# The first merge of DeltaNet's block inverse, done in 32x32 pieces on four row and column groups

## The chip, the cores and the metric

The kernel runs on one core of a Trainium2 chip. The metric is the device time of one launch in microseconds (us). Five engines of the core matter here: TensorE (PE for the matmul, PEld for loading its weights), VectorE (DVE), ScalarE (ACT), GpSimd (POOL) and SyncE (SP), which issues DMAs. Each works through its own list of instructions in order; semaphores tie them together. The time before the change is 1111.03 us, the median of 3 runs (1110.56 to 1111.17).

## The reference, cut to what matters

The program is a two-layer decoder trunk over 272 tokens (16 learned ones, 256 of the input) of width 1024: six sub-layers, four of them SwiGLU, one mixer of retention and gated DeltaNet heads, one of windowed and stick-breaking attention. The change is in the DeltaNet part of the first mixer. There the chunks of 64 tokens need the solution of a unit lower triangular system for each of four heads:

```python
a_mat = jnp.where(strict, jnp.einsum('bnhid,bnhjd->bnhij', k_beta, k) * decay, 0.0)
system = a_mat + jnp.eye(C, dtype=a_mat.dtype)
rhs = jnp.concatenate([v * beta[..., None], k_beta * jnp.exp(g_cum)[..., None]], axis=-1)
sol = lax.linalg.triangular_solve(system, rhs, left_side=True, lower=True, unit_diagonal=True)
```

and a scan over chunks that uses `sol`.

## The kernel before, in words

The kernel processes the DeltaNet tokens in chunks of 128 instead of 64, and inverts the triangular matrices instead of solving. Two chunks times four heads give eight matrices of 128x128 (index `q` from 0 to 7; a ninth holds the 16 last tokens of all heads). The 16x16 blocks on the diagonal are inverted on DVE (`block_inverses`). Then three merges double the block: 16 to 32 (`m == 0`), 32 to 64 (`m == 1`), 64 to 128 (`m == 2`). With X the inverse so far and E the part of the matrix that lies between two neighbouring blocks, a merge forms E·X (`merge_first`, PE), copies it from PSUM to the SBUF tile `w1` (`merge_copy`, ACT; `w1` is the buffer `dN`), forms X·(E·X) (`merge_second`, PE), and brings that into X (for `m == 0` an addition on DVE in `first_merged`, for the others a copy on ACT). The tile `XX` holds X in `XX[:, 0]` and its transpose in `XX[:, 1]`; DVE's 32x32 block transposes (`transposed`) make the second from the first.

In the first merge each of the eight matrices takes one matmul of 128x128 by 128x128 per product. `off_diag` is the matrix with a mask that leaves the 16x16 blocks E, so that all of the other entries multiplied are zeros. The results fill two PSUM banks for each product (4 and 5, then 6 and 7), four matrices in each. The second merge is already done in pieces of 32x32 (two for each matrix), whose results lie side by side in one bank (`merge_ps(1, bank)` is [128, 8, 32]; `merge_w1(1)` the same shape in `w1`).

The order of the work is written out by hand, one list for each engine. PE's list alternates projections (`proj(n, m)`: half a chunk of the mixer's input projection, 24 matmuls of 128x128 by 128x272, lines 1772 to 1774) and small DeltaNet matmuls (helper `mm`, line 1877), so that the second wait on other engines behind the first:

```python
proj(11, 0); merge_first(0); proj(11, 1); merge_second(0)
proj(12, 0); merge_first(1); proj(12, 1); merge_second(1)
proj(13, 0); merge_first(2); proj(13, 1)
```

A projection's weights are f32 and split in two parts: ACT makes the high part (`hi`, line 704), DVE the low part (`lo`, line 1153, 2.3 us each); `proj(n, 0)` waits for the low part of its chunk. DVE's list around the change is `start_inverse`, `off_diagonal`, `transposed(0, 9)`, `rotate(0)`, `lo(b + 12)`, `rotate(1)`, `first_merged()`, `conv(4)`, `lo(b + 13)`, `rotate(2)`, `conv(5)`, `second_merged()`, `rotate(3)`, `evac(12)`, `lo(b + 14)`, two small steps, `evac(13)`. ACT's is `raw_copy(2)`, `merge_copy(0)`, `hi(b + 13)`, `merge_copy(1)`, `conv_silu(4)`, `tap(5)`, `raw_copy(3)`, `merge_result(1)`. `rotate` is line 1281 to 1284, `conv` line 1270, `raw_copy` line 833, `evac` line 1259.

Of the kernel before, what the change touches and what calls it, by code (L numbers as in the profile page):

```python
# [24 lines left out]
ALU = mybir.AluOpType  # L25
# [122 lines left out]
def build(nc, a, c, out):  # L148
# [18 lines left out]
    with ctx:  # L167
# [311 lines left out]
        def blocks(bank, lo_, hi_):  # L479

            return ps[:, bank, 0:(hi_ - lo_) * P].rearrange("p (n c) -> p n c", c=P)
# [212 lines left out]
        def _(act):  # L694
# [98 lines left out]
            def ab(k, b):  # L793
# [41 lines left out]
                def merge_copy(m):  # L835

                    if m == 0:
                        for g, (lo_, hi_) in enumerate(GROUPS[:2]):
                            act.wait_ge(s_w1, g + 1)
                            act.activation(w1[:, lo_:hi_, :], blocks(4 + g, lo_, hi_), ACT.Copy).then_inc(s_w1c, 1)  # L840
                        return
                    act.wait_ge(s_w1, 2 + m)
                    for r in ((slice(TAIL, 2 * TAIL), slice(3 * TAIL, P)), (slice(P // 2, P),))[m - 1]:
                        ins = act.activation(merge_w1(m)[r, :, :], merge_ps(m, 3 + m)[r, :, :], ACT.Copy)
                    ins.then_inc(s_w1c, 1)

                def merge_result(m):

                    act.wait_ge(s_w2, 2 + m)
                    if m == 1:  # L850
                        for r, c0 in ((slice(TAIL, 2 * TAIL), 0), (slice(3 * TAIL, P), 2 * TAIL)):
                            ins = act.activation(XX[r, 0, 0:8, c0:c0 + TAIL], merge_ps(1, 6)[r, :, :], ACT.Copy)
                        ins.then_inc(s_X1, 1)
                    else:
                        act.activation(XX[0:P // 2, 1, 0:8, P // 2:P], merge_ps(2, 7)[0:P // 2, :, :], ACT.Copy).then_inc(s_X2, 1)
# [286 lines left out]
        def _(dve):  # L1142
# [105 lines left out]
            def ab(k, b):  # L1248
# [92 lines left out]

                def first_merged():

                    for g, (lo_, hi_) in enumerate(GROUPS[:2]):
                        dve.wait_ge(s_w2, g + 1)
                        dve.tensor_tensor(XX[:, 0, lo_:hi_, :], XX[:, 0, lo_:hi_, :], blocks(6 + g, lo_, hi_), ALU.add)\
                            .then_inc(s_T, 1)
                    for g, (lo_, hi_) in enumerate(GROUPS[:2]):
                        dve.wait_ge(s_T, g + 1)
                        transposed(lo_, hi_)  # L1350

                def second_merged():
# [407 lines left out]
        def _(pe):  # L1760
# [115 lines left out]
            def mm(o, lhsT, rhs, start=True, stop=True):  # L1876
                return pe.matmul(o, lhsT, rhs, start=start, stop=stop, skip_group_check=True)  # L1877

            def ab(k, b):
# [4 lines left out]
                def col(bank, q):  # L1884
                    return ps[:, bank, q % 4 * P:(q % 4 + 1) * P]
# [18 lines left out]
                def merge_first(m):  # L1904

                    if m == 0:
                        for g, (lo_, hi_) in enumerate(GROUPS[:2]):
                            pe.wait_ge(s_E, g + 1)
                            pe.wait_ge(s_X0, g + 1)
                            for q in range(lo_, hi_):  # L1910
                                ins = mm(col(4 + g, q), off_diag[:, q, :], XX[:, 0, q, :])
                            ins.then_inc(s_w1, 1)
                        return
                    n = (TAIL, 2 * TAIL)[m - 1]
                    pe.wait_ge(s_T, 2) if m == 1 else pe.wait_ge(s_X1, 1)
                    for q in range(8):
                        for r in range(0, P, 2 * n):
                            ins = mm(merge_ps(m, 3 + m)[r + n:r + 2 * n, q, :], dmat[r:r + n, q, r + n:r + 2 * n],
                                     XX[r:r + n, 0, q, r:r + n])
                    ins.then_inc(s_w1, 1)  # L1920

                def merge_second(m):

                    if m == 0:
                        pe.wait_ge(s_XT, 1)
                        for g, (lo_, hi_) in enumerate(GROUPS[:2]):
                            pe.wait_ge(s_w1c, g + 1)
                            for q in range(lo_, hi_):
                                ins = mm(col(6 + g, q), XX[:, 1, q, :], w1[:, q, :])
                            ins.then_inc(s_w2, 1)  # L1930
                        return
                    pe.wait_ge(s_w1c, 2 + m)
                    pe.wait_ge(s_XT, 3 if m == 1 else 4)
                    for q in range(8):
                        if m == 1:
                            for r in (TAIL, 3 * TAIL):
                                ins = mm(merge_ps(1, 6)[r:r + TAIL, q, :], XX[r:r + TAIL, 1, q, r:r + TAIL],
                                         merge_w1(1)[r:r + TAIL, q, :])
                        else:
                            ins = mm(merge_ps(2, 7)[0:P // 2, q, :], merge_w1(2)[P // 2:P, q, :], XX[P // 2:P, 1, q, P // 2:P])  # L1940
                    ins.then_inc(s_w2, 1)
# [483 lines left out]
```

## Time and profile before

| | us |
|---|---|
| median of 3 runs | 1111.03 |
| lowest and highest | 1110.56, 1111.17 |
| profiled execution | 1110.44 |
| its span, first to last instruction | 1108.5 |
| PE busy in it | 1091.3 |
| DVE busy | 703.4 |
| ACT busy | 544.5 |
| mean granted TensorE clock | 0.999 of full |

The span is what the trace covers; the other 1.9 us of the profiled execution lie around it. Busy times are sums over the span; a busy engine need not be the one that others wait for in a given stretch. The work of the change lies between 294 and 329 us of the span. In rows of PE one fp32 matmul of the program shows as two records (x16 for eight matmuls), and a record's length includes the time that it shares with its neighbours in the pipeline, so that the step from one start to the next tells the rate.

### The profile page before, as it was taken

Reading aid. Unit: us, or ns where it says so; the run is one execution under the profiler, and the core shown is the slowest. Engines: PE = TensorE matmul, PEld = TensorE weight load, DVE = VectorE, ACT = ScalarE, POOL = GpSimd, SP = SyncE. Lnnn points to the kernel's source line nnn. Section 1 sums busy time; section 2 is a strip of 40 time slices with the busy share of each in tenths; the row PEclk is TensorE's granted clock in tenths of the full one; section 3 lists DMA queues with packets and bytes.
Section 4 is the critical chain, followed back from the end, with each engine's and each line's share of the span. In section 5 each row is a group of like instructions: output and inputs, shape, how many; then the busy total and the mean of one; then the engine's idle time right before and its main releaser. Section 6 shows DMA issues by size and latency. Waiting matters only on the chain.

```text
span 1108.5 us, 19363 instructions
## 1 busy us (share of the span) xinstructions
PE 1091.3 (98%) x8597; PEld 1060.2 (96%) x8597; DVE 703.4 (63%) x770; ACT 544.5 (49%) x633; POOL 1.6 (0%) x13
## 2 busy tenths in 40 slices
PE   9999999999999999999999999999999999999998
PEld 8999999999988999999999999999999899999986
DVE  6755654588996667665547665564477867666542
ACT  5544343466545655433445534344465766544441
POOL 0000000000000000000000000000000000000000
PEclk9999999999999999999999999999999999999999
DMA  9566556857741445555453655555653244556551
GB/s 320 181 188 181 178 171 160 161 111 184 162 150 38 128 143 186 167 176 174 160 188 126 194 186 169 164 176 176 191 172 119 77 143 157 182 180 199 168 171 39
DMA packets 173072, 180.02 MB, mean 162 GB/s; under 512 B 7508, under 2 KB 165804, under 8 KB 172988
## 3 DMA queue, kind: packets, MB, share of 16 engines
q1 hardware_dynamic: 172668, 177.66, 53.3%
q8 instruction: 68, 1.11, 0.4%
q10 hardware_dynamic: 320, 1.11, 0.3%
q14 instruction: 16, 0.13, 0.0%
HBM read 177.05 MB, written 1.71 MB: 161 GB/s over the span
## 4 chain that ended last, share of the span: by engine, by line
PE 88%; DVE 7%; ACT 3%; issue 1%; DMA 1%; ACTq 0%; DVEq 0%
PE ps L1772 24%; PE ps L1774 23%; PE ps L1773 23%; PE ps L1877 4%; PE ps L1862 2%; PE ps L1861 2%; PE ps L1860 2%; PE ps L1995 2%; PE ps L1806 1%; PE ps L1809 1%; DVE w_lo L1153 1%; PE ps L1810 1%; PE ps L1844 1%; DVE hT L1202 1%; DVE yT L1201 1%
## 5 line engine op out<-in xcount | busy, mean ns | idle before, releaser
L1772 PE MATMUL ps<-u_hi,w_hi 128*128 128x272 f32 (+1 forms) x1656 | 479.9, 290 | 3.1 <-DVE w_lo L1153 1.2
L1774 PE MATMUL ps<-u_hi,w_lo 128*128 128x272 f32 (+1 forms) x1656 | 476.4, 288 | 0.0
L1773 PE MATMUL ps<-u_lo,w_hi 128*128 128x272 f32 (+1 forms) x1656 | 474.4, 286 | 0.0
L1153 DVE TENSOR_TENSOR w_lo<-raw,w_hi 128x2048 fp32r<-128x2048 f32 (+2 forms) x167 | 369.5, 2235 | 113.8 <-ACT w_hi L704 113.8
L704 ACT ACTIVATE w_hi<-raw 128x2048 fp32r<-128x2048 f32 (+2 forms) x167 | 310.6, 1869 | 168.2 <-PE ps L1774 143.7
L1772 PEld LDWEIGHTS ps<-u_hi,w_hi 128*128 128x128 f32 x1656 | 311.9, 188 | 5.5 <-ACT attn L967 1.2
L1773 PEld LDWEIGHTS ps<-u_lo,w_hi 128*128 128x128 f32 x1656 | 311.9, 188 | 0.3
L1774 PEld LDWEIGHTS ps<-u_hi,w_lo 128*128 128x128 f32 x1656 | 311.9, 188 | 0.0
L1772 PE MATMUL ps<-hid_hi,w_hi 128*128 128x272 f32 x528 | 152.1, 288 | 0.0
L1773 PE MATMUL ps<-hid_lo,w_hi 128*128 128x272 f32 x528 | 152.0, 288 | 0.0
L1774 PE MATMUL ps<-hid_hi,w_lo 128*128 128x272 f32 x528 | 151.5, 287 | 0.0
L1171 DVE TENSOR_TENSOR prod<-gates,ps 128x544 f32<-128x544 f32 (+1 forms) x44 | 31.4, 712 | 164.6 <-PE ps L1774 160.0
L711 ACT ACTIVATE gates<-gates 128x544 f32<-128x544 f32 (+1 forms) x44 | 28.7, 653 | 158.0 <-DVE gates L1161 158.0
L1774 PEld LDWEIGHTS ps<-hid_hi,w_lo 128*128 128x128 f32 x528 | 99.4, 188 | 0.0
L1772 PEld LDWEIGHTS ps<-hid_hi,w_hi 128*128 128x128 f32 x528 | 99.3, 188 | 0.0
L1773 PEld LDWEIGHTS ps<-hid_lo,w_hi 128*128 128x128 f32 x528 | 99.2, 188 | 0.0
L1809 PE MATMUL ps<-u_hi,w_hi 128*128 128x272 f32 (+1 forms) x160 | 41.3, 292 | 2.6 <-ACT u_hi L768 2.2
L1161 DVE TENSOR_TENSOR gates<-ps,rstd 128x544 f32<-128x544 f32 (+1 forms) x44 | 31.4, 713 | 18.7 <-ACT rstd L744 13.9
L1810 PE MATMUL ps<-u_hi,w_lo 128*128 128x272 f32 (+1 forms) x160 | 40.4, 287 | 0.0
L717 ACT ACTIVATE hid_hi<-prod 128x544 fp32r<-128x544 f32 (+1 forms) x44 | 28.0, 635 | 24.2 <-DVE prod L1172 24.2
L1862 PE MATMUL ps<-w_hi,hid_lo 128*128 128x512 f32 x88 | 34.7, 394 | 0.0
L1860 PE MATMUL ps<-w_hi,hid_hi 128*128 128x512 f32 x88 | 34.6, 393 | 0.0
(350 smaller groups left out, 1053.0 us busy)
## 6 DMA issues: line engine op xcount, KB each, us to landing
raw<-ffn_w_up SPq DMA_DIRECT2D x44, 1024.0 KB, 5.4
raw<-ffn_w_gate SPq DMA_DIRECT2D x43, 1024.0 KB, 5.4
raw<-ffn_w_down SPq DMA_DIRECT2D x24, 896.0 KB, 4.9
raw<-ffn_w_down SPq DMA_DIRECT2D x20, 1024.0 KB, 5.2
raw<-ab_w_in SPq DMA_DIRECT2D x16, 1024.0 KB, 14.2
raw<-cd_w_in SPq DMA_DIRECT2D x9, 1024.0 KB, 5.4
raw<-ab_w_out SPq DMA_DIRECT2D x4, 1024.0 KB, 7.4
raw<-cd_w_out SPq DMA_DIRECT2D x4, 1024.0 KB, 5.1
```

Source lines behind the costliest of these rows:

```text
L704: act.activation(w_hi[:, n % NW, 0:rows(n) * CB], raw[:, n % NR, 0:rows(n) * CB], ACT.Copy)\
L1153: dve.tensor_tensor(dst, src, w_hi[:, n % NW, 0:rows(n) * CB].bitcast(F32), ALU.subtract)\
L1161: dve.tensor_tensor(gates[:, j % 2, :, tok], two(pair_banks(j), tok), rstd_two(1, tok), ALU.mult)\
L1171: step.done(dve.tensor_tensor(to, gates[:, j % 2, :, tok], two(pair_banks(j) + 2, tok), ALU.mult))
L1772: pe.matmul(o, wh, rhs_hi[:, kk, tok], start=first and kk == 0, stop=False)
L1773: pe.matmul(o, wh, rhs_lo[:, kk, tok], start=False, stop=False)
L1774: ins = pe.matmul(o, wl, rhs_hi[:, kk, tok], start=False, stop=last and kk == rows(n) - 1)
L1809: pe.matmul(o, wh, u_hi[:, kk, tok], start=kk == 0, stop=False, skip_group_check=True)
L1810: pe.matmul(o, wl, u_hi[:, kk, tok], start=False, stop=False, skip_group_check=True)
L1860: pe.matmul(o, hid_hi[:, kk, tok], wh, start=kk == 0, stop=False, skip_group_check=True)
L1862: ins = pe.matmul(o, hid_lo[:, kk, tok], wh, start=False, stop=kk == KF - 1, skip_group_check=True)
L1877: return pe.matmul(o, lhsT, rhs, start=start, stop=stop, skip_group_check=True)
```

## The change

The first merge is done as the second is. Of each matrix only the four 32x32 blocks on the diagonal are multiplied, one for each of TensorE's four row groups (partitions 0, 32, 64, 96) and the column group of the same number. Results of all eight matrices lie side by side in one PSUM bank ([128, 8, 32]; bank 5 for E·X, bank 7 for X·(E·X)). ACT copies 128x256 once instead of 128x512 twice. DVE adds the result into the four diagonal blocks of `XX[:, 0]`, one instruction for each group of 32 partitions (32x256), where it had one for each four matrices (128x512). Two semaphore counts fall to one, and later waits on them are lowered by one.

```diff
 def merge_copy(m):                                    # ACT
     if m == 0:
-        for g, (lo_, hi_) in enumerate(GROUPS[:2]):
-            act.wait_ge(s_w1, g + 1)
-            act.activation(w1[:, lo_:hi_, :], blocks(4 + g, lo_, hi_), ACT.Copy).then_inc(s_w1c, 1)
+        act.wait_ge(s_w1, 1)
+        act.activation(merge_w1(1), merge_ps(1, 5), ACT.Copy).then_inc(s_w1c, 1)
         return
-    act.wait_ge(s_w1, 2 + m)
+    act.wait_ge(s_w1, 1 + m)
...
 def first_merged():                                   # DVE
-    for g, (lo_, hi_) in enumerate(GROUPS[:2]):
-        dve.wait_ge(s_w2, g + 1)
-        dve.tensor_tensor(XX[:, 0, lo_:hi_, :], XX[:, 0, lo_:hi_, :], blocks(6 + g, lo_, hi_), ALU.add)\
-            .then_inc(s_T, 1)
-    for g, (lo_, hi_) in enumerate(GROUPS[:2]):
-        dve.wait_ge(s_T, g + 1)
+    dve.wait_ge(s_w2, 1)
+    for r in range(0, P, TAIL):
+        own = slice(r, r + TAIL)
+        ins = dve.tensor_tensor(XX[own, 0, 0:8, own], XX[own, 0, 0:8, own], merge_ps(1, 7)[own, :, :], ALU.add)
+    ins.then_inc(s_T, 1)
+    dve.wait_ge(s_T, 1)
+    for lo_, hi_ in GROUPS[:2]:
         transposed(lo_, hi_)
...
 # merge_first(0)                                      # PE
             for q in range(lo_, hi_):
-                ins = mm(col(4 + g, q), off_diag[:, q, :], XX[:, 0, q, :])
-            ins.then_inc(s_w1, 1)
+                for r in range(0, P, TAIL):
+                    own = slice(r, r + TAIL)
+                    ins = mm(merge_ps(1, 5)[own, q, :], off_diag[own, q, own], XX[own, 0, q, own])
+        ins.then_inc(s_w1, 1)
...
 # merge_second(0)                                     # PE
-        for g, (lo_, hi_) in enumerate(GROUPS[:2]):
-            pe.wait_ge(s_w1c, g + 1)
-            for q in range(lo_, hi_):
-                ins = mm(col(6 + g, q), XX[:, 1, q, :], w1[:, q, :])
-            ins.then_inc(s_w2, 1)
+        pe.wait_ge(s_w1c, 1)
+        for q in range(8):
+            for r in range(0, P, TAIL):
+                own = slice(r, r + TAIL)
+                ins = mm(merge_ps(1, 7)[own, q, :], XX[own, 1, q, own], merge_w1(1)[own, q, :])
+        ins.then_inc(s_w2, 1)
```

No step is moved in any list; the line numbers above the DVE part fall by one. On DVE, at `first_merged`, between the second rotation and the convolution, there stands before (bracketed names are the semaphores that an instruction waits for):

```order
L1283 TENSOR_TENSOR yT<-yT,rope 128x544
L1284 TENSOR_TENSOR yT<-yT,rot 128x544 [waits dve_step]
L1346 TENSOR_TENSOR XX<-XX,ps 128x512 [waits merge_products,rotated]
L1346 TENSOR_TENSOR XX<-XX,ps 128x512 [waits merge_products]
L1340 STREAM_TRANSPOSE XX<-XX 128x512 [waits merge_done] x2
L1270 SCALAR_TENSOR_TENSOR cacc<-gv,convw,cacc 128x271 [waits conv_first_tap]
```

and now, in the same place:

```order
L1282 TENSOR_TENSOR yT<-yT,rope 128x544
L1283 TENSOR_TENSOR yT<-yT,rot 128x544 [waits dve_step]
L1346 TENSOR_TENSOR XX<-XX,ps 32x8x32 [waits merge_products,rotated]
L1346 TENSOR_TENSOR XX<-XX,ps 32x8x32 x3
L1339 STREAM_TRANSPOSE XX<-XX 128x512 [waits merge_done]
L1339 STREAM_TRANSPOSE XX<-XX 128x512
L1269 SCALAR_TENSOR_TENSOR cacc<-gv,convw,cacc 128x271 [waits conv_first_tap]
```

Two additions have become four, and the first transpose now waits for the last addition instead of the first. On PE, at `merge_first(0)`, between the two halves of projection 11, there stands before:

```order
L1774 MATMUL ps<-u_hi,w_lo 128x272
L1877 MATMUL ps<-XX,off_diag 128x128 [waits inverse_started,off_diagonal_ready,qk_decayed]
L1877 MATMUL ps<-XX,off_diag 128x128 x3
L1877 MATMUL ps<-XX,off_diag 128x128 [waits inverse_started,off_diagonal_ready]
L1877 MATMUL ps<-XX,off_diag 128x128 x3
L1772 MATMUL ps<-u_hi,w_hi 128x272
```

and now:

```order
L1774 MATMUL ps<-u_hi,w_lo 128x272
L1877 MATMUL ps<-XX,off_diag 32x32 [waits inverse_started,off_diagonal_ready,qk_decayed]
L1877 MATMUL ps<-XX,off_diag 32x32 x15
L1877 MATMUL ps<-XX,off_diag 32x32 [waits inverse_started,off_diagonal_ready]
L1877 MATMUL ps<-XX,off_diag 32x32 x15
L1772 MATMUL ps<-u_hi,w_hi 128x272
```

Eight matmuls have become 32 in the same place behind the same waits; `merge_second(0)` changes alike.

## Rows read from the trace of the kernel before

**Rows 1.** The page: busy us, share of the span and instructions of each engine.
```profile
PE 1091.3 (98%) x8597; PEld 1060.2 (96%) x8597; DVE 703.4 (63%) x770; ACT 544.5 (49%) x633; POOL 1.6 (0%) x13
```
**Rows 2.** The page: the chain that ended last, shares of the span by engine.
```profile
PE 88%; DVE 7%; ACT 3%; issue 1%; DMA 1%; ACTq 0%; DVEq 0%
```
**Rows 3.** PE's waits from 290 to 345 us: us in total, times, longest us.
```profile
PE ps L1877 <- ACT dN L844: 0.8, 1, 0.8
PE ps L1877 <- ACT rv_tok L956: 0.8, 1, 0.8
PE ps L1772 <- DVE w_lo L1153: 0.7, 1, 0.7
PE ps L1772 <- DVE rg L1259: 0.5, 1, 0.5
```
**Rows 4.** One stretch: length, busy us (instructions) by engine, granted clock, DMA share, GB/s.
```profile
core 0: us, PE busy (x) PEld busy (x) DVE busy (x) ACT busy (x) POOL busy (x), PEclk, DMA share, GB/s
294.70:329.00 34.30, 32.28 (x324) 30.56 (x324) 33.61 (x54) 13.48 (x19) 0.00 (x0) 1.00 0.68 182
```
**Rows 5.** DVE's waits from 294.8 to 329 us, in full.
```profile
DVE dT L1481 <- PE ps L1877: 1.0, 1, 1.0
```
**Rows 6.** Timeline of PE: start us, us, engine, line, operation, count, [idle before, releaser].
```profile
300.78 1.95 PE L1877 MATMUL ps<-XX,off_diag 128*128 128x128 f32 x16
302.48 0.37 PE L1772 MATMUL ps<-u_hi,w_hi 128*128 128x272 f32 x1
...
305.58 1.95 PE L1877 MATMUL ps<-dN,XX 128*128 128x128 f32 x16
307.29 0.37 PE L1772 MATMUL ps<-u_hi,w_hi 128*128 128x272 f32 x1
...
310.26 0.29 PE L1774 MATMUL ps<-u_hi,w_lo 128*128 128x272 f32 x1
310.48 0.69 PE L1877 MATMUL ps<-XX,dmat 32*32 32x32 f32 x32
311.10 0.39 PE L1772 MATMUL ps<-u_hi,w_hi 128*128 128x272 f32 x1
...
314.32 0.69 PE L1877 MATMUL ps<-dN,XX 32*32 32x32 f32 x32
315.72 0.36 PE L1772 MATMUL ps<-u_hi,w_hi 128*128 128x272 f32 x1 [0.71 <-DVE w_lo L1153]
```
**Rows 7.** Timeline of DVE in the same stretch.
```profile
307.43 0.72 DVE L1284 TENSOR_TENSOR yT<-yT,rot 128x544 f32<-128x544 f32 x1
308.19 1.28 DVE L1346 TENSOR_TENSOR XX<-XX,ps 128x512 f32<-128x512 f32 x2
309.39 1.29 DVE L1340 STREAM_TRANSPOSE XX<-XX 128x512 f32<-128x512 f32 x2
...
313.29 2.28 DVE L1153 TENSOR_TENSOR w_lo<-raw,w_hi 128x2048 fp32r<-128x2048 f32 x1
...
321.28 0.89 DVE L1356 STREAM_TRANSPOSE XX<-XX 32x256 f32<-32x256 f32 x2
```
**Rows 8.** DVE's groups by form: busy us, mean ns | idle us before.
```profile
L1346 DVE TENSOR_TENSOR XX<-XX,ps 128x512 f32<-128x512 f32 x2 | 1.3, 682 | 0.0
L1191 DVE TENSOR_TENSOR ss<-ss,y_sq 128x256 f32<-128x256 f32 x3 | 1.3, 421 | 0.7 <-ACT y_sq L737 0.7
L1632 DVE TENSOR_TENSOR kdup<-ps,rstd 64x272 f32<-64x272 f32 x4 | 1.8, 438 | 3.1 <-PE ps L1774 3.1
```
**Rows 9.** Timeline of DVE at line 1632, in the second mixer.
```profile
834.95 1.79 DVE L1632 TENSOR_TENSOR kdup<-ps,rstd 64x272 f32<-64x272 f32 x4 [3.08 <-PE ps L1774]
```
**Rows 10.** Timeline of ACT in the stretch of the change.
```profile
302.76 0.60 ACT L840 ACTIVATE dN<-ps 128x512 f32<-128x512 f32 x1 [0.30 <-PE ps L1877]
...
311.22 0.77 ACT L844 ACTIVATE dN<-ps 32x256 f32<-32x256 f32 x2 [6.06 <-PE ps L1877]
```
**Rows 11.** The end of the span, columns as in Rows 4.
```profile
1099.50:1103.50 4.00, 3.56 (x16) 2.55 (x14) 1.74 (x4) 1.50 (x5) 0.00 (x0) 1.00 0.01 2
1103.50:1106.00 2.50, 0.00 (x0) 0.00 (x0) 2.46 (x5) 0.69 (x4) 0.00 (x0) 1.00 0.56 210
1106.00:1108.50 2.50, 0.00 (x0) 0.00 (x0) 0.05 (x1) 0.00 (x0) 0.00 (x0) 0.65 0.56 210
```

More of the change, by code:

```diff
@@ L847, in merge_result @@
                 def merge_result(m):
-                    act.wait_ge(s_w2, 2 + m)
+                    act.wait_ge(s_w2, 1 + m)
                     if m == 1:
@@ L1910, in merge_first @@
                             for q in range(lo_, hi_):
-                                ins = mm(col(4 + g, q), off_diag[:, q, :], XX[:, 0, q, :])
-                            ins.then_inc(s_w1, 1)
+                                for r in range(0, P, TAIL):
+                                    own = slice(r, r + TAIL)
+                                    ins = mm(merge_ps(1, 5)[own, q, :], off_diag[own, q, own], XX[own, 0, q, own])
+                        ins.then_inc(s_w1, 1)
                         return
                     n = (TAIL, 2 * TAIL)[m - 1]
-                    pe.wait_ge(s_T, 2) if m == 1 else pe.wait_ge(s_X1, 1)
+                    pe.wait_ge(s_T, 1) if m == 1 else pe.wait_ge(s_X1, 1)
                     for q in range(8):
@@ L1925, in merge_second @@
                         pe.wait_ge(s_XT, 1)
-                        for g, (lo_, hi_) in enumerate(GROUPS[:2]):
-                            pe.wait_ge(s_w1c, g + 1)
-                            for q in range(lo_, hi_):
-                                ins = mm(col(6 + g, q), XX[:, 1, q, :], w1[:, q, :])
-                            ins.then_inc(s_w2, 1)
+                        pe.wait_ge(s_w1c, 1)
[4 more added lines that the diff above has]
+                        ins.then_inc(s_w2, 1)
                         return
-                    pe.wait_ge(s_w1c, 2 + m)
+                    pe.wait_ge(s_w1c, 1 + m)
                     pe.wait_ge(s_XT, 3 if m == 1 else 4)
```

## The prediction, made before the changed kernel was run

> **What bounds the kernel now.** I read the page's busy line first: PE is busy 98% of the span and DVE 63% [rows 1]. By that a kernel that takes work off PE gains what it takes off. The chain of waits says nearly the same for the whole span, 88% PE and 7% DVE [rows 2], but shares over six sub-layers don't tell who is last where the change is. So I looked at the stretch of the DeltaNet inverse alone. From 294.70 to 329.00 us DVE is busy 33.61 of 34.30 us and PE 32.28 [rows 4]. Its one wait, 1.0 us for the matmuls of line 1877 [rows 5], ends where the stretch begins; the 0.69 us that are missing from the stretch are the hundredths between instructions that depend on each other. So DVE does not stop until 329. PE does: 0.7 us for DVE's low part of chunk 13 (line 1153), at 315.72, and 0.5 us for DVE's scaling of line 1259 at the end of the stretch, with 0.8 us for ACT's copy of line 844 between them [rows 3, 6]. That copy stands in ACT's list behind a SiLU that waits for DVE's convolution, so it moves with DVE too. Seen as a race, DVE runs from 294.76 to 329 without rest, and PE, although the busier engine of the whole kernel, waits for it at three places. The end is set here by DVE; from 329 on PE carries the chain.
>
> **The change on PE.** It removes two sets of eight 128x128 matmuls. The first takes 302.48 - 300.78 = 1.70 us from its first start to the next projection's, the second 307.29 - 305.58 = 1.71 us [rows 6]. It adds two sets of 32 matmuls of 32x32, 64 records each. The second merge shows that kind already: 16 matmuls, 32 records, in 311.10 - 310.48 = 0.62 us, and a lead-in: projection matmuls start 0.126 us apart, the last at 310.26, so the next could have started at 310.39 and did at 310.48, 0.09 us lost at the change of shape [rows 6]. Those 16 use two row groups at a time. If four groups run side by side as two do, 64 records take the same 0.62 us and a set costs 0.71; if only two ever overlap, it costs 1.24 + 0.09 = 1.33. PE saves 1.0 us a set by the first and 0.4 by the second. I take the first, 2.0 us in all, because the two groups that the row shows belong to different row and column groups, as the four will.
>
> Here a rule speaks against the change. The Trainium skill, "TensorEngine Tiling (Array Packing)", section "Restrictions and Gotchas", says that different row tiles cannot access the same PSUM bank at the same time, and the change puts four of them on one bank. The trace does not bear it out for two: rows 0 and 64 write bank 4 in turn in the second merge, at 0.62 us for 32 records, 19 ns each [rows 6], where a record of the 128x128 kind takes 1.70 / 16 = 106 ns. By the rule taken strictly there would be no overlap at all; what that would cost is a rival below.
>
> What becomes of PE's 2.0 us? Nothing: PE comes to `merge_first(1)` at about 310.39 - 2.0 = 308.4 us, and that waits for DVE's additions, which end near 309.9 as worked out next. It starts some 1.6 us late. Then 0.62 us, a projection half of 3.2 us and 0.7 us of `merge_second(1)` bring it to 314.5, and `proj(13, 0)` waits again for DVE's line 1153, some 1.7 us instead of 0.71. The cover that swallows the gain is DVE's list, and the same cover would swallow a loss: PE could lose 0.71 us before anyone noticed.
>
> **The change on ACT.** Two copies of 128x512, 0.60 us each, become one of 128x256. A copy of 32x256 takes about 0.38 us (0.77 for two) [rows 10]; copies on this engine are paid by elements of a partition, so I take 0.38. It can only start when all 32 matmuls are done, about 301.5, and ends near 301.9, where the second old one ended at 303.36; PE wants it at 305.58 - 1.0, about 304.6 [rows 6]. No one waits for it. ACT's conversion for chunk 13 follows it earlier, and DVE reads that at 313.29 [rows 7], 8 us later. Cost nothing; if the cover of PE's half projection (3.1 us) were gone, the single copy would be in the way by 0.4 us.
>
> **The change on DVE, which decides.** Before, two additions of 128x512 run from 308.19, and the first transpose starts at 309.39: 1.20 us [rows 7]. Its semaphore had long been raised by the first addition, so it started 0.08 us before the second ended: 308.19 + 1.28 = 309.47. Now four additions of 32 partitions by 256 elements stand there, and the transposes wait for the last. The elements per partition are as many as before, 4 x 256 = 2 x 512; the fixed part of an instruction is paid four times instead of twice. One addition of 128x256 takes 0.421 us, one of 128x512 0.682 [rows 8]. That 32 partitions are no cheaper than 128 I read from the transposes of 32x256 in the second merge, 0.89 / 2, about 0.44 each [rows 7], and from the 64-partition multiplication of line 1632, 0.438 for 272 elements [rows 8].
>
> How closely do they follow each other? Full-width neighbours overlap by 1.28 - 2 x 0.682 = -0.08 us. Line 1632 does not: four of 0.438 take 1.79 us, so 1.79 - 4 x 0.438 = +0.04, a gap of 0.013 each [rows 8, 9]; the two transposes of line 1356 take 0.89 for two also [rows 7]. Both are instructions that begin on another partition than the one before. So four additions take 4 x 0.421 + 3 x 0.013 = 1.72, and behind them a waiting instruction starts some 0.04 late (307.43 + 0.72 to 308.19 [rows 7]): 1.76 us. With the 1.20 taken off, DVE is **0.56 us later** from here on. Bounds: if the four overlapped as full-width ones do, 4 x 0.421 - 3 x 0.08 + 0.04 = 1.48, +0.28 us. If each is as slow as the 32-partition transposes with their step of 0.45, 3 x 0.45 + 0.44 + 0.04 = 1.83, +0.63 us. Below nothing it can't go, as even the overlapped four are longer. I take 0.56, as line 1632 is the same operation with PSUM as a source and changing partitions.
>
> The Trainium skill has this as a rule: "VectorE: DVE Perf Modes", section "Two Vector instructions with no wait between them", holds an instruction until all before it are finished when its input or output begins in another group of 32 partitions than the last one's. By it the second, third and fourth addition are held (+0.56), and without it they would overlap (+0.28); this trace agrees with it at line 1632.
>
> **The sum.** PE 2.0 us saved, off the path: 0. ACT 0. DVE +0.56, on the path: from 308.19 to 329.00 DVE has no idle time to absorb it [rows 4, 5], at 329.00 PE is waiting for it, and afterwards PE and ACT start from there. Profiled execution 1110.44 + 0.56 = 1111.0 (span 1108.5 to 1109.1). The median of the runs stands 0.59 above the profiled one; the change laid on it gives 1111.03 + 0.56 = 1111.6 us.
>
> **Rivals.**
> 1. *The additions overlap after all*: +0.28, 1111.3 us. For it: full-width ones do. Against: line 1632.
> 2. *The 0.56 is absorbed later*: 1111.0 us. After 329 PE waits 0.8 us for ACT's line 956 [rows 3]; if ACT were bound by something of its own, not shifted, DVE's delay could vanish there. Against: that copy waits for PE's own matmuls.
> 3. *PE's saving reaches the end*: 1111.03 - 2.0 = 1109.0 us (1110.2 with the smaller saving). It needs DVE to have slack in the stretch. For it: PE is 98% busy overall [rows 1]. Against: rows 4 and 5.
> 4. *The row groups take turns at the bank*, the strict rule: with 64 records of 0.106 us a set is 6.8 us, 5.1 more than now; two sets 10.2, less the 0.71 + 0.56 that PE may be late at `proj(13, 0)`, gives about +9.5 with the 0.56: 1120.5 us. It decides once a set takes more than 1.70 + 0.64 = 2.3 us. Against it: the 19 ns record step of the second merge.
> 5. *The clock falls* (slower): the change gives PE two idle gaps of 1.6 and 1.7 us within 8 us, where the longest in this part are 0.8 us [rows 3]. The granted clock was full (2.4 GHz) in every stretch in which PE worked, also in a stretch of 2.50 us without any matmul, and fell towards the other level, 1.2 GHz, only after that (mean 0.65) [rows 11]. If it fell at 316, `proj(13, 0)` would take twice its 3.1 us: +3.1 + 0.56, 1114.7 us. Against: neither gap is longer than that stretch which kept the clock, and a projection half stands between them.
>
> **Numbers.** Forecast 0.70; rival 1 0.12; rival 2 0.06; rival 3 0.05; rival 4 0.03; rival 5 0.04. The predicted time is the forecast's, 1111.6. The range takes in rivals 1 and 2, the upper bound (+0.63) and the scatter of the runs before (0.6 us from lowest to highest): 1110.5 to 1112.4. A measurement of this kernel can tell about 0.2% from no change, 2.2 us; the forecast and rivals 1 to 3 all lie inside that (rival 3 just: 2.0 us). Faster by more than that 0.02, within it 0.91, slower 0.07 from rivals 4 and 5.
>
> **What would show it.** In the profile after: both sets on PE at about 0.7 us; four additions of about 0.42 us that do not overlap, and the first transpose 1.7 to 1.8 us after the first addition; PE waiting some 1.6 us ahead of `merge_first(1)` and some 1.7 us ahead of `proj(13, 0)`; DVE without idle time up to PE's wait for line 1259, and that start near 329.6. PE's busy time falls by about 2 us while the span grows. The prediction is wrong if DVE shows idle time between the additions and 329, if a set takes over 2.3 us, or if the granted clock drops in the stretch.

## The result, and the profile after

The changed kernel takes 1112.72 us (median of 20 runs, 1110.69 to 1117.02); the kernel before, measured beside it, 1110.74 (20 runs, 1110.41 to 1112.02). The ratio is 1.0019, 95% interval 1.0012 to 1.0026: slower by 2.0 us, which as a ratio is just inside the 0.2% that counts as no change, though the interval reaches past it. The forecast was 1111.6 with a range to 1112.4, so the median lies outside it. The same kernel was measured twice more, beside experiments 5 to 8 and 9 to 11, and took 1111.01 and 1111.08 us there: the 2.0 us are not a fixed price of the change, and what follows is about why they came once. The profiled execution took 1112.37 us, its span is 1110.6, where the kernel before has 1108.5.

First what came as forecast. The page's first part and its instruction queue (packets, MB, share of the 16 DMA engines):

```profile
PE 1092.2 (98%) x8693; PEld 1060.7 (96%) x8693; DVE 704.3 (63%) x772; ACT 543.8 (49%) x632; POOL 1.6 (0%) x13
...
q8 instruction: 68, 1.11, 0.4%
```

PE has 96 matmul records and 96 weight loads more than in [rows 1]. Its timeline at the two sets, columns as in rows 6:

```profile
301.13 0.75 PE L1877 MATMUL ps<-XX,off_diag 32*32 32x32 f32 x64
301.81 0.39 PE L1772 MATMUL ps<-u_hi,w_hi 128*128 128x272 f32 x1
...
305.03 0.75 PE L1877 MATMUL ps<-dN,XX 32*32 32x32 f32 x64
305.73 0.37 PE L1772 MATMUL ps<-u_hi,w_hi 128*128 128x272 f32 x1
...
306.32 0.29 PE L1773 MATMUL ps<-u_lo,w_hi 128*128 128x272 f32 x1
310.71 0.38 PE L1774 MATMUL ps<-u_hi,w_lo 128*128 128x272 f32 x1 [4.10 <-issue]
310.89 0.43 PE L1772 MATMUL ps<-u_hi,w_hi 128*128 128x272 f32 x1
...
314.70 0.69 PE L1877 MATMUL ps<-XX,dmat 32*32 32x32 f32 x32
...
318.55 0.69 PE L1877 MATMUL ps<-dN,XX 32*32 32x32 f32 x32
```

A set takes 301.81 - 301.13 = 0.68 and 0.70 us with 0.09 ahead of it; 1.70 and 1.71 before [rows 6]. So PE saves 2.0 us. It came to the first set 0.35 us later than before in this execution (301.13 for 300.78), and is back at the projection at 305.73, 1.56 us ahead of the 307.29 of [rows 6]. DVE's and ACT's timelines, columns as in rows 7:

```profile
308.46 1.71 DVE L1346 TENSOR_TENSOR XX<-XX,ps 32x256 f32<-32x256 f32 x4
310.21 1.31 DVE L1339 STREAM_TRANSPOSE XX<-XX 128x512 f32<-128x512 f32 x2
...
314.12 2.28 DVE L1152 TENSOR_TENSOR w_lo<-raw,w_hi 128x2048 fp32r<-128x2048 f32 x1
...
331.13 0.72 DVE L1363 TENSOR_TENSOR attn<-ps,decay 128x544 f32<-128x544 f32 x1 [0.17 <-PE ps L1877]
...
337.14 0.72 DVE L1363 TENSOR_TENSOR attn<-ps,decay 128x544 f32<-128x544 f32 x1 [2.63 <-PE ps L1877]
```
```profile
301.93 0.39 ACT L839 ACTIVATE dN<-ps 128x256 f32<-128x256 f32 x1 [3.09 <-PE ps L1877]
```

From the first addition to the first transpose pass 310.21 - 308.46 = 1.75 us (1.76 forecast, 1.20 before [rows 7]), and the copy takes 0.39 (0.38 forecast).

Then what nobody had forecast: PE stands still for 4.10 us from 306.6 to 310.71, in the middle of a projection. The reason given is `issue`: it waits for no engine that the profile shows. It is PE's only wait from 290 to 345 us:

```profile
PE ps L1774 <- issue: 4.1, 1, 4.1
```

The waits for DVE and for ACT's copy [rows 3] are gone (the one for `rv_tok` has moved behind 345 us): PE is now the late one. Stretches, columns as in rows 4:

```profile
298.00:301.00 3.00, 3.00 (x26) 2.98 (x24) 3.00 (x5) 0.63 (x1) 0.00 (x0) 1.00 1.01 257
301.00:304.00 3.00, 3.00 (x83) 2.83 (x82) 2.90 (x5) 2.07 (x2) 0.00 (x0) 1.00 1.02 217
304.00:306.30 2.30, 2.30 (x77) 2.11 (x76) 2.28 (x3) 0.12 (x1) 0.00 (x0) 1.00 0.69 188
306.33:310.71 4.38, 0.28 (x3) 0.19 (x2) 4.24 (x8) 0.00 (x0) 0.00 (x0) 1.00 0.90 290
310.74:314.16 3.42, 3.42 (x16) 3.42 (x16) 3.35 (x9) 0.00 (x0) 0.00 (x0) 0.50 0.21 72
314.16:318.00 3.84, 3.84 (x58) 3.65 (x58) 3.81 (x6) 2.50 (x6) 0.00 (x0) 1.00 0.01 3
```

Right behind the pause the granted clock is 0.50 (1.2 GHz) for 3.42 us; projection matmuls are then 0.227 us apart (310.89 to 311.12 and so on) instead of 0.126, 15 steps at 0.10 more, 1.5 us. The sum on PE: -1.56 + 4.26 (4.38 from 306.33 to 310.71, less a normal step) + 1.5 = +4.2 us. `proj(13, 0)` begins at 319.18; before it began at 315.72 after a wait of 0.71 [rows 6], and 4.2 - 0.71 is the 3.46 between the two. The two waits behind it (0.8 for dN, 0.5 for rg [rows 3]) swallow 1.3, and some 2.1 are left. DVE's second `attn` piece confirms it: it starts at 337.14, and in the kernel before at 335.12. Without the stop the forecast's 0.56 would be the whole of it, so 1.5 are new. Experiment 1, the changed kernel without the stop, bears that out: there the piece starts at 335.72.

**Why PE stood still.** The queue called instruction moved 68 packets and 1.11 MB, 16 KB each. PE has 2 x 8693 = 17,386 records of matmuls and weight loads by the page; at 256 to a block those are 67.9 blocks, so the packets are PE's own instructions, 64 bytes each. (That every record has its instruction in them I infer from these two numbers. Experiment 5, with 120 records more, bears it out: 17,506 are 68.4 blocks, and it has 69 packets.)

Which record a block begins with shows in the trace too. Counting the 160 records of PE's sequencer as well (17,546 in all; the numbers of records from here on count them), PE stops in front of record 5057. With a border every 256 records before and behind that one there are 68 borders for the 68 packets, and the packets start at a median of 1.3 us before PE comes to the border of the same number. So a block is fetched about when PE comes to one border and is needed at the next. The block that begins with record 5057 was due when PE came to record 4801, at 301.38.

That packet lies in the pause. The DMA view of two short stretches of the changed kernel (q1 is the data, q8 the instructions: packets, MB, share of 16 engines) shows it:

```profile
q1 hardware_dynamic: 1389, 1.40, 82.9%
raw<-ab_w_out SPq DMA_DIRECT2D x1, 1024.0 KB, 10.0
...
q1 hardware_dynamic: 351, 0.36, 101.0%
q8 instruction: 1, 0.02, 5.9%
```

The first two rows are 301.2 to 308.2: seven microseconds of weight loads and no instruction packet. The last two are 308.2 to 309.2: the packet moves, among loads that fill all 16 engines, for 5.9% x 16 x 1.0 = 0.94 us. In the kernel before the corresponding packet moves in 308.28 to 309.21, just as late; the view of its stretch from 308.2 to 309.3 has

```profile
q8 instruction: 1, 0.02, 5.3%
```

PE, though, stood at its record 4871 then in the kernel before and was supplied up to 5057, which it reached at 314.66. The changed kernel puts 192 records more in front (in two sets 64 matmul records for 16, each with its weight load) and does the work earlier: it reaches record 5057 at 306.33 and has nothing to execute until 310.71, 1.5 us after the packet ended. What stood in front of the packet: two loads of ab_w_in, 1 MB each, were issued from 291.27 on and two of ab_w_out at 298.21 and 305.13, and the DMA engines are full from 298 to 304 (share 1.01 and 1.02 above). That the loads hold the packet up is tested below (experiments 1, 9 and 11). How they do isn't shown: from 304.5 to 308.0 the mean share is only 0.63, and the packet still doesn't move.

### The profile page after: what moved, and what is told of

Read it like the earlier page. It is cut to its first block, busy times and chain, and to the rows that moved or that the text cites. A ratio compares the mean times of both kernels' runs of the same rounds, so it can differ in the third digit from the quotient of the medians.

```text
span 1110.6 us, 19556 instructions
## 1 busy us (share of the span) xinstructions
PE 1092.2 (98%) x8693; PEld 1060.7 (96%) x8693; DVE 704.3 (63%) x772; ACT 543.8 (49%) x632; POOL 1.6 (0%) x13
## 3 DMA queue, kind: packets, MB, share of 16 engines
q8 instruction: 68, 1.11, 0.4%
q10 hardware_dynamic: 320, 1.11, 0.2%
HBM read 177.05 MB, written 1.71 MB: 161 GB/s over the span
## 4 chain that ended last, share of the span: by engine, by line
PE 91%; DVE 4%; ACT 3%; issue 1%; DMA 1%; ACTq 0%; DVEq 0%
PE ps L1772 24%; PE ps L1774 24%; PE ps L1773 24%; PE ps L1877 5%; PE ps L1862 2%; PE ps L1861 2%; PE ps L1860 2%; PE ps L1998 2%; PE ps L1806 1%; PE ps L1809 1%; PE ps L1810 1%; PE ps L1844 1%; DVE hT L1201 1%; DVE yT L1200 1%; DVE w_lo L1152 1%
```

## Experiments

**Theory S**: PE's supply of instructions ran out, since the block stood behind the weight loads; it takes more records and earlier work on PE, and loads on the DMA engines when the block is due. **Rival K**: the kind of matmul (32x32 on four groups) makes the pause. **Rival Q**: it belongs to that one execution. The time apart from it is DVE's +0.56. Ratios are to the kernel before, measured beside each kernel: 1110.47 us beside experiments 1 to 4, 1110.48 beside 5 to 8, 1110.50 beside 9 to 12.

**1. Loads of ab_w_out later.** The changed kernel with one line:

```
+                    sp.wait_ge(s_w2, 1)
                     for i in range(NBLK):          # the loads of ab_w_out
```

> The changed kernel with one wait more on SP: the four loads of the mixer's output weights (the first issued at 298.21 us) are held until merge_second(0) is done, about 306. Nothing else differs. Theory S (supply): in the changed kernel PE stands still 4.1 us from 306.6 because its own instructions are missing. They come in blocks of 16 KB (queue q8), the block wanted near 301 moved only at 308.24, behind the weight loads, and PE had run out of what it held at 306.33 as the change puts 192 more records ahead of that point. With the load out of the way the block moves by about 303, PE has no idle of the kind 'issue', the clock stays full, and only DVE's +0.56 us is left: ratio to the kernel before 1.0005, profiled time 1111.0. Theory K (kind): the pause is caused by the four-group matmuls themselves; it stays at about 4 us and the ratio at 1.0019.

1110.98 us (1110.89 to 1111.32 in 11 runs), ratio 1.0004 (0.9995 to 1.0012). Its profile's PE waits:

```profile
PE ps L1773 <- DVE w_lo L1153: 1.8, 1, 1.8
PE ps L1878 <- DVE XX L1347: 1.2, 1, 1.2
PE ps L1878 <- ACT dN L844: 0.8, 1, 0.8
```

No `issue`; the waits of rows 3 are back, and the two that the prediction named (1.6 and 1.7 us) are there at 1.2 and 1.8. The block moved at 302.03, before the loads. The runs lie within 0.43 us, those of the changed kernel's first measurement within 6.3 and of its two later ones within 1.8. The median is that of the kernel before, 1110.47, plus 0.51. The unedited kernel was not measured beside this one, and reached the same median in experiments 6 and 12, so that the profile shows the effect of the edit and the median alone doesn't.

**2. DVE's part alone.** The kernel before with its 128x128 matmuls, and four additions over the diagonal blocks (`both` is banks 6 and 7 as one tile):

```
-  for g ... dve.tensor_tensor(XX[:, 0, lo_:hi_, :], XX[:, 0, lo_:hi_, :], blocks(6 + g, lo_, hi_), ALU.add)
+  dve.wait_ge(s_w2, 2)
+  for r in range(0, P, TAIL): own = slice(r, r + TAIL)
+      dve.tensor_tensor(XX[own, 0, 0:8, own], XX[own, 0, 0:8, own], both[own, :, own], ALU.add)
```

> The kernel before with DVE's part of the change alone: PE multiplies 128x128 and ACT copies as before, but DVE adds the diagonal 32x32 blocks in four instructions of 32x256, one for each 32 partitions. This computes the same result. Both theories: no pause on PE, additions take 1.75 us instead of 1.20, ratio 1.0005 (+0.56 us). If DVE's part were the larger share of the measured +2.0 us, the ratio would be near 1.0015.

1111.00 us, ratio 1.0005 (0.9996 to 1.0014): +0.53 on 1110.47, no pause. DVE's timeline has the additions as in the changed kernel:

```profile
308.84 1.71 DVE L1348 TENSOR_TENSOR XX<-XX,ps 32x256 f32<-32x256 f32 x4
310.58 1.31 DVE L1340 STREAM_TRANSPOSE XX<-XX 128x512 f32<-128x512 f32 x2
```

The term of 0.56 stands, by itself.

**3. More records of the tiled kind.** The kernel before with 48 idle 32x32 matmuls behind `merge_first(0)`, 192 records of matmuls and loads of them in a row:

```
+                        for q in range(12):
+                            for r in range(0, P, TAIL):
+                                own = slice(r, r + TAIL)
+                                mm(merge_ps(1, 7)[own, q % 8, :], off_diag[own, q % 8, own], XX[own, 0, q % 8, own])
```

> The kernel before with its 128x128 merge, and 48 matmuls of 32x32 (192 records, as many as the change adds) put behind merge_first(0); their results land in a bank that merge_second(0) overwrites, so the output is the same. DVE and ACT as before. Theory S: PE uses up its instructions at record 5057, which it reaches about 309.0 (307.9 in the kernel before at record 4865, and 1.1 us for the added ones), and goes on at about 310.7 when the block has landed: a pause of about 1.7 us, at that record and nowhere else; ratio 1.001 to 1.002. Theory K: a pause of about 4 us within 1.5 us behind the added matmuls, near 304.5.

1110.38 us, ratio 1.0002 (0.9993 to 1.0011), no pause:

```profile
PE ps L1877 <- ACT rv_tok L956: 0.8, 1, 0.8
PE ps L1772 <- DVE rg L1259: 0.5, 1, 0.5
PE ps L1877 <- ACT dN L844: 0.4, 1, 0.4
```

K is refuted: the same kind of matmul in the same place, and no stop (nor in 1 and 5, which have the change's own). S missed too, as it had expected a pause of 1.7 us: in this execution the loads of ab_w_in were issued at 289.22, 2.2 us earlier than in the kernel before, and the block moved at 305.21 instead of 308. That was the first sign that the time of the block is not fixed by the kernel. It also shows PE's cover: over 1 us of added work took the place of the wait for w_lo and half of that for dN [rows 3], at no cost.

**4. The second set alone** tiled (with DVE's part), half the records:

```
-  ins = mm(col(6 + g, q), XX[:, 1, q, :], w1[:, q, :])
+  ins = mm(merge_ps(1, 7)[own, q, :], XX[own, 1, q, own], w1[own, q, own])      # four, own = 32 rows each
```

> Half of the change: merge_first(0) and the two copies as before, merge_second(0) in 32x32 pieces on four groups, DVE's additions as in the change. It adds 96 records instead of 192 and computes the same result. Theory S: record 5057 is reached about 310 to 311, when the block that moved at 308.28 has landed or nearly: pause under 0.7 us, ratio 1.0005 from DVE's part. Theory K: the pause comes behind the one set that is left, at full size or half of it (2 to 4 us), ratio 1.001 or more.

1111.04 us, ratio 1.0006 (0.9997 to 1.0015), no pause; its block moved at 306.49 and PE came to record 5057 only at 311.02. The same as the change without the pause, so the PE saving of the first set indeed brings nothing.

**5. The block asked for earlier.** The changed kernel with 120 records more at about 214 us, which moves the borders of the blocks against the work:

```
-                for _ in range(8):
+                for _ in range(8 if k else 6):      # and 32 matmuls of 32x32 on ones and ident behind them, at k == 0
```

> The changed kernel with its merge and its loads untouched, and 120 more PE records some 87 us ahead of it: at 214 us, where PE waits for ACT, two of the eight 128x128 matmuls that keep it busy give way to 32 of 32x32 (results unused). This moves all later places at which PE asks for its next 16 KB of instructions forward by 120 records. Theory S: the block that was asked for near 301.2, behind the weight load issued at 298.21, is asked for near 295, ahead of it; it moves by 302 (when the two loads issued at 291.3 are through), while PE's supply now ends near 305. No pause, ratio 1.0005, profiled 1111.0. Theory K (the four-group matmuls pause PE by themselves): 4 us pause as before. A theory that any surplus of records in this part is too much for the fetches: pause near 305, longer than 4 us as the supply ends earlier.

1110.98 us, ratio 1.0005 (0.9996 to 1.0013), no pause, although the loads of ab_w_in were issued late (293.40): PE came to the border at 298.01, before the load of ab_w_out at 298.84, and the block moved at 299.81, even before the 302 expected. The merge and the loads are as in the changed kernel; what has changed is where the border of a block falls. The profiled execution took 1111.87 and not 1111.0.

That profile and those of 2 and 4 have spans of 1110.1, 1109.8 and 1109.7 us without a pause, where experiment 1 has 1109.1. In them DVE takes up `blk_x` (the inverted blocks, read back from DRAM) at 297.06, 296.81 and 296.74, and at 296.18 in experiment 1: a late `blk_x` is a second source of scatter, of up to 1 us here.

**6. The changed kernel again**, beside 5, 7 and 8.

> The changed kernel once more, beside the others on one chip. Theory S: a pause of kind 'issue' again after PE's record 5057, of a length that goes with the moment at which its block moves on q8; time about 2 us over the kernel before, with a wide scatter. A theory that the first profile was an accident: 1111.0 and no pause.

1111.01 us (1110.75 to 1112.56), ratio 1.0005 (0.9996 to 1.0014). The 2 us that S expected are missing; here it gives the forecast's time. Its profile has the stop at the same record, 5057, but the block had moved by 305.22:

```profile
306.66 0.29 PE L1774 MATMUL ps<-u_hi,w_lo 128*128 128x272 f32 x1 [0.32 <-issue]
309.88 0.69 PE L1877 MATMUL ps<-XX,dmat 32*32 32x32 f32 x32 [0.67 <-DVE XX L1346]
```

The loads were issued at 289.84, 1.4 us before those of the first profile. They stand in SP's list behind the way of the block inverses through DRAM (line 635 waits until the store has landed), and that landing varies from one execution to the next. The moment of issue doesn't fix the block's time by itself: in experiment 12 the loads were issued at 289.50, earlier still, and the block moved at 306.19, 2.6 us later than here.

**7. The mask on GpSimd.** To see whether DVE's list is what bounds, the kernel before with the two multiplications by the off-diagonal mask moved from DVE to GpSimd:

```
+                    pool.wait_ge(s_ATc, 3)
+                    for lo_, hi_ in GROUPS[:2]:
+                        pool.tensor_tensor(off_diag[:, lo_:hi_, :], dmat[:, lo_:hi_, :], mask(MERGE, 4), ALU.mult).then_inc(s_E, 1)
```

> The kernel before with its two masks of off_diagonal (128x512 each, 1.21 us of DVE's list) done on GpSimd, which is idle there and has dmat from about 275 us on; computes the same. If DVE's list is what sets the end from 294.76 to 329 us (PE waits 2.0 us for it in three places), the kernel gains 1.2 us: ratio 0.9989. If PE were the bound there, at most the 0.7 us of its first wait; if GpSimd slows DVE on the shared port, less, or a loss.

1110.09 us (1109.74 to 1114.16), ratio 1.0000 (0.9991 to 1.0009). A miss in size: -0.4 instead of -1.2, and the profiled execution (1112.89) isn't like the median one. Inconclusive.

**8. Late loads and the mask on GpSimd** in the changed kernel, the combination that the first results pointed to:

> The changed kernel with the late loads of e1_load_late (no pause) and the masks on GpSimd as in e7_mask_on_pool. Theory S with a DVE-bound stretch: +0.56 - 1.21 = -0.65 us against the kernel before, 1109.8 us, ratio 0.9994; 0.5 us slower than e7_mask_on_pool, since PE's saving is again under the cover of DVE. If PE's 2 us counted once DVE is shorter, it would be the fastest of all, near 1108.5.

1110.57 us (1110.27 to 1111.02), ratio 0.9999 (0.9990 to 1.0008): 0.4 under experiment 1, as fast as the kernel before, not faster; 1109.8 was expected. PE's wait in its timeline, and the stretch behind it:

```profile
315.60 0.36 PE L1775 MATMUL ps<-u_hi,w_hi 128*128 128x272 f32 x1 [1.79 <-DVE w_lo L1157]
```
```profile
315.85:319.26 3.41, 3.41 (x17) 3.41 (x17) 3.28 (x6) 2.26 (x2) 0.00 (x0) 0.50 0.53 187
```

Right behind PE's wait the clock is at half for 3.4 us, and PE has no wait for dN or rg any more. It cost next to nothing all the same: DVE's additions start at 307.52 (308.23 in experiment 1), 0.71 us earlier, and its second `attn` piece at 335.05 (335.72), 0.67 earlier. The rest of the 1.2 us is missing ahead of the additions, as DVE took up `blk_x` 0.38 us later in this execution. The clock fell for 3.4 us in 4 and 5 too, from 318.3 on, behind the same wait of 1.8 and 1.7 us, and not in 1 and 6 with 1.8. So the wait alone doesn't decide it; what does is open.

Up to here a long pause was seen in one execution and was absent from others. The next experiment makes it.

**9. Loads in the way.** The changed kernel with the last two loads of ab_w_in held back until blk_x has landed:

```
 sp.dma_start(blk_x[:, :, :], ...).then_inc(s_iload, 16)
+sp.wait_ge(s_iload, 16)
```

> The changed kernel, with the two last loads of ab_w_in (1 MB each, issued 291.27 in its first profile) held back until the load of blk_x has landed, some 3 us later; they are needed only from about 316 us. Nothing on PE, DVE or ACT is edited. Theory S (PE's instructions come in blocks of 256 records on the queue named instruction, behind the weight loads; the block that starts at record 5057 of the stretch is asked for near 301.2 and must be there at 306.3): the block comes at 308 us or later, so PE stops at the same record after 306.3, a pause of 4 us or more (row `<- issue` on the line of the projection), the granted clock halves behind it, and the time is 2 to 4 us above the changed kernel without a pause: 1112.9 to 1115 where that is 1111.0, ratio to before 1.002 to 1.004. Rival Q (the pause is something of that one execution and not of the order on the DMA engines): no pause, 1111.0, ratio 1.0005. Rival W (the loads themselves are late for their readers): PE or DVE waits for ACT's w_hi for raw, no `<- issue` row.

1112.86 us (1110.69 to 1116.30), ratio 1.0027 (1.0016 to 1.0038): the slowdown of the first measurement, back, its scatter too, while the unedited changed kernel took 1111.08 beside it (12). The profiled execution is one of the shorter, 1111.66. PE's timeline, and q1 and q8 from 307.6 to 308.7:

```profile
310.14 0.38 PE L1775 MATMUL ps<-u_hi,w_lo 128*128 128x272 f32 x1 [3.55 <-issue]
```
```profile
q1 hardware_dynamic: 385, 0.39, 102.1%
q8 instruction: 1, 0.02, 5.3%
```

The loads were issued at 291.43 here, and the block moved at 307.70. The clock is at half from 309.81 to 313.21, and no wait for ACT's `w_hi` shows, so rival W is out. The pause was to be 4 us or more and is 3.6: in this execution blk_x had been issued at 289.11, so that the hold added about 2 us instead of 3.

**10. The same two loads held back in the kernel before.**

> The kernel before with the same two loads held back. Theory S: 192 records fewer stand in the stretch, so PE has instructions until about 314.7 us; a block that comes at 308 to 311 us is in time. No `<- issue` pause, 1110.5, ratio 0.9995 to 1.0005. Rival W (the loads are late for their readers): as slow here as in the changed kernel, 1112 or more. If the block came even later than 314 us, a short pause of up to 2 us would show near 314.7.

1110.67 us (1110.28 to 1111.27), ratio 1.0001 (0.9992 to 1.0009). The loads are issued still later, at 294.10, the block moves at 307.39, and PE waits as in rows 3:

```profile
PE ps L1878 <- ACT dN L845: 0.8, 1, 0.8
PE ps L1878 <- ACT rv_tok L957: 0.8, 1, 0.8
PE ps L1773 <- DVE w_lo L1154: 0.7, 1, 0.7
PE ps L1773 <- DVE rg L1260: 0.5, 1, 0.5
```

So the hold costs next to nothing by itself (0.2 us, within the interval), and a block at 307 to 308 us hurts only the kernel that has used up its instructions by then.

**11. Held back in both places**, the loads of ab_w_in as in 9 and those of ab_w_out as in 1.

> The changed kernel with the two ab_w_in loads held back as in the first, and in addition the ab_w_out loads held back until the first merge is done (about 306 us), so that they don't stand between the request of the block and its arrival. Theory S: the block's 16 KB only has 2 MB in front of it, and comes at 303 to 306 us: the pause is gone or at most 0.6 us, time 1111.0 to 1111.3, ratio 1.0005. Rival Q: no difference to the first. If the ab_w_in loads alone keep the DMA engines full until 308, the pause stays at 2 us or more.

1111.03 us (1110.61 to 1111.42, and one of 1115.03), ratio 1.0004 (0.9996 to 1.0013). The time is as expected; the pause is not gone, but down to 1.6 us, since the ab_w_in loads alone (issued 292.78) kept the block until 305.74. That was mis-sized by a microsecond. Against 9, from which it differs by the one wait in front of the ab_w_out loads and beside which it was measured, the median is 1.8 us lower.

**12. The changed kernel a third time**, beside 9 to 11.

> The changed kernel as it is, for the third time. Theory S: its time depends on when the block moves, which the kernel does not fix: 1111.0 where it comes before about 305, up to 1112.7 where it comes at 308. From its profile alone the two must go together: a row `<- issue` of 3 to 4 us with a block that moved near 308, or none (or under 0.6 us) with one that moved by 305.5.

1111.08 us (1110.78 to 1112.62), ratio 1.0007 (0.9999 to 1.0016). The pause is there, 2.5 us with a block at 306.19, between the two cases that the expectation names, and costs nothing in this execution:

```profile
308.60 0.29 PE L1774 MATMUL ps<-u_hi,w_lo 128*128 128x272 f32 x1 [2.45 <-issue]
...
329.40 0.39 PE L1772 MATMUL ps<-u_hi,w_hi 128*128 128x272 f32 x1 [0.41 <-DVE rg L1258]
```

PE still waits for DVE's line 1258 at 329.40, so whatever it lost has been absorbed, half clock (308.97 to 312.38) included. The executions beside each other; block times are those of the 16 KB packet in the trace:

| profile | ab_w_in issued | block moved | PE out of instructions | resumes | `issue` | span |
|---|---|---|---|---|---|---|
| before | 291.45 | 308.28-309.21 | would be 314.66 | - | 0 | 1108.5 |
| changed, first | 291.27 | 308.24-309.18 | 306.33 | 310.71 | 4.1 | 1110.6 |
| 9, in the way | 291.43 | 307.70-308.64 | 306.31 | 310.14 | 3.6 | 1109.9 |
| 12, third | 289.50 | 306.19-307.12 | 305.87 | 308.60 | 2.5 | 1109.0 |
| 11, both late | 292.78 | 305.74-306.70 | 306.02 | 307.94 | 1.6 | 1109.1 |
| 6, again | 289.84 | 303.57-305.22 | 306.05 | 306.66 | 0.3 | 1109.0 |
| 1, ab_w_out late | 291.26 | 302.03-303.32 | - | - | 0 | 1109.1 |

In all five that stop (the changed kernel's three, 9 and 11), PE stops at the same record, 5057, and resumes 1.2 to 1.5 us after the packet's end. Up to 2.5 us of pause the span is that of the change without a pause; 3.6 costs 0.8 us and 4.1 costs 1.5. Each is one execution. By estimate PE can lose 2.0 us saved + 2.0 of waits in rows 3 that are bound to DVE + 0.56 by which DVE is later, less 1.5 for the half clock: about 3 us of pause, as the spans have it. S holds; Q is refuted by 9, K by 3.

## Why the prediction was wrong

- *What bounds*: right. DVE works from 294.76 on without rest, PE waits for it wherever PE isn't stopped (experiments 1, 6), and what is added to its list reaches the end in full (+0.53 us in experiment 2). Of the 1.2 us taken off its list only 0.4 show in the medians (7, and 8 against 1); experiment 7 was inconclusive, and why the medians gain no more is open.
- *PE, 2.0 us saved*: right to 0.1 us. Four row groups on one bank run as two do, 64 records in 0.68 us. The rule of the Trainium skill, "TensorEngine Tiling (Array Packing)", "Restrictions and Gotchas", that different row tiles cannot access one PSUM bank at the same time, shows no price here; rival 4 is out.
- *ACT, nothing*: right, 0.39 us and nobody waited.
- *DVE, +0.56*: right, 1.75 us for 1.76 in the profile and +0.53 us in experiment 2. The four are held apart, as the rule of the Trainium skill, "VectorE: DVE Perf Modes", "Two Vector instructions with no wait between them", has it; rival 1 is out.
- *What becomes of PE's 2.0 us: "Nothing", and "PE could lose 0.71 us before anyone noticed"*: **this is the step that failed.** It counted PE's 192 added records at nothing as long as their duration was hidden, with no term for their being fetched, and took it for granted that PE can execute whatever is ready. In the first measurement PE used the time gained, and 192 records more, to reach the end of its supply 8 us early, at 306.33 instead of 314.66, before the next block had come through the weight loads: +4.26 us of pause, +1.5 of half clock. Against that stood what PE was ahead and the waits behind. Together +1.5 us in the profiled execution. Whether the step costs anything is chance, as the kernel doesn't fix when the block moves: in the two later measurements the same kernel took 1111.01 and 1111.08, +0.5 and +0.6 us, as forecast. The absorbing capacity itself was larger than I said: with the gain it is about 3 us of pause.
- *Rival 5, the clock falls*: it fell, which was one of the signs of being wrong, but behind a cause that the rival didn't name, and it cost 1.5 us of PE and not 3.1. Behind the gap of 1.7 us ahead of `proj(13, 0)`, the one it feared, the clock stayed full in experiments 1 and 6 and was at half for 3.4 us in 4, 5 and 8. There the waits for dN and rg took it up: from the additions to the second `attn` piece DVE needs 27.50 us in 4 and 27.54 in 5, as in experiment 1 (27.49). So its argument against a fall, that a gap of 2.50 us had kept the clock [rows 11], didn't hold, and its price of 3.1 us didn't come.
- *The base*: the kernel before measured 1110.74 in place of 1111.03; with the forecast's +0.56 that makes 1111.3, so 1.4 us of the measured 1112.72 are the missing term. In the seven measurements with DVE's four additions in which the profiled execution has no pause or a short one (1, 2, 4, 5, 6, 11, 12) the ratio is 1.0004 to 1.0007; the forecast's is 0.56 / 1111 = 1.0005.

Open: the runs of up to 1117.02 us (granted clock down to 0.995 over the span, 0.998 in the profiled one) are longer than any profiled one. That they are the same pause with longer or repeated half clock is likely by experiment 9, five of whose 11 runs took 1114.8 to 1116.3, while those of 10 ended at 1111.27; no profile shows one.

## What to carry to other kernels

Splitting a matmul into many small ones costs instructions even where it saves time: count the records between two `q8 instruction` packets, and look at what fills the DMA queues when the next block is due. A busy PE at the edge of its supply shows in the profile of before as a packet that is late and yet not missed. If an engine is going to be faster in a stretch with full DMA engines, hold back the loads that nobody needs yet; one wait on SP's list took the stop out of the profile and left the runs of the changed kernel 0.4 us apart at +0.5 us (1), and took 1.8 us off the kernel that had the other loads in the way (11 against 9).

## What was new of the hardware

- PE's instructions travel as 16 KB packets, 256 records each, on the same 16 DMA engines as the data. The packets of the table took 0.9 to 1.6 us to move, and where PE had stopped it went on 1.2 to 1.5 us behind the packet's end.
- Behind weight loads a packet due at 301.38 us moved at 308.24, 6.9 us later; with the loads of ab_w_out away, one due at 301.13 moved at 302.03.
- 64 records of 32x32 matmuls on four row and column groups and one PSUM bank take 0.68 to 0.70 us, 11 ns each; on two groups 32 take 0.62 [rows 6].
- With each stop of PE of 4.1, 3.6, 2.5 and 1.6 us came some 3.4 us at the lower clock (1.2 GHz, granted 0.50), which began between 0.3 us before and 0.4 us after PE went on; the one of 0.3 us had none. A wait of 1.7 to 1.8 us was followed by it in experiments 4, 5 and 8, and wasn't in 1 and 6.
